# Moving the operands of the small matmuls by 64 bytes in SBUF

## The reference

```
x = x + hgrn2(rmsnorm(x))            # gated linear recurrence, 16 heads of 128, blocks by levels
k, v, F = shared_kv(x)               # keys, values, cumulative forget gates
x = x + fox(rmsnorm(x), k, v, F)     # softmax(q k^T / sqrt(128) + F[t] - F[s], causal) v
h = rmsnorm(x)
x = x + (sigmoid(gr) * rg_lru(conv(h W)) + sigmoid(ga) * dsa_attention(...)) @ w_o
x = x + peer(rmsnorm(x))             # 8 heads, 16 of 128*128 experts each, u[e].x -> gelu -> v[e]
out = rmsnorm(x)
```

## Time and profile before

| | us |
|---|---|
| median of 3 runs | 3218.08 (3217.72 to 3223.16) |
| the profiled execution | 3218.28 |
| its span, first to last instruction | 3216.3 |
| PE busy in the span | 3187.9 (99%), 25285 matmuls |
| DVE busy | 2365.6 (74%) |
| ACT busy | 1686.9 (52%) |
| mean granted TensorE clock | 0.997 |

### The profile page before, as it was taken

One profiled execution on the slowest core, in us unless ns is written; L12 is line 12 of the kernel. 1 busy time (PEld: TensorE's weight loads), 2 busy tenths in 40 slices (PEclk: granted clock), 3 DMA queues, 4 the chain that ended last, 5 costly groups with the idle time before them and its releaser, 6 DMA issues.

```text
span 3216.3 us, 63027 instructions
## 1 busy us (share of the span) xinstructions
PE 3187.9 (99%) x25285; PEld 3028.9 (94%) x25285; DVE 2365.6 (74%) x3779; ACT 1686.9 (52%) x2284; POOL 33.4 (1%) x46
## 2 busy tenths in 40 slices
PE   8999999999999999999999999999999999999998
PEld 8999999999999999999999999998899889987887
DVE  8767667656566776566669998975699558999865
ACT  5444455767775656555544444444444444444444
POOL 4000000000000000000000000000000000000000
PEclk9999999999999999999999999999999999999999
DMA  5444445444445544545454555555555555555554
GB/s 185 159 155 161 152 158 196 158 157 167 161 168 184 190 171 160 189 161 189 169 186 171 185 190 183 181 192 191 190 184 183 195 190 186 181 180 182 183 209 157
DMA packets 99095, 569.94 MB, mean 177 GB/s; under 512 B 9456, under 2 KB 30320, under 8 KB 31600
## 3 DMA queue, kind: packets, MB, share of 16 engines
q1 hardware_dynamic: 98784, 567.06, 49.9%
q10 hardware_dynamic: 144, 0.52, 0.0%
HBM read 565.45 MB, written 2.10 MB: 176 GB/s over the span
## 4 chain that ended last, share of the span: by engine, by line
PE 89%; DVE 7%; DVEq 1%; ACT 1%; issue 1%; DMA 1%; ACTq 0%; POOL 0%; POOLq 0%; SPq 0%
PE bank L583 20%; PE bank L584 20%; PE bank L585 20%; PE bank L1105 7%; PE bank L1107 7%; PE bank L1106 7%; DVE wl L1668 3%; PE bank L1029 1%; PE bank L737 1%; PE bank L940 0%; PE bank L815 0%; PE bank L814 0%; ACT wh L1162 0%; PE bank L686 0%; DMA raw<-w_out_b 0%
## 5 line engine op out<-in xcount | busy, mean ns | idle before, releaser
L584 PE MATMUL bank<-hl,wh 128*128 128x256 f32 x5616 | 1556.9, 277 | 0.0
L583 PE MATMUL bank<-hh,wh 128*128 128x256 f32 x5488 | 1540.5, 281 | 2.8 <-DVE wl L1668 1.7
L585 PE MATMUL bank<-hh,wl 128*128 128x256 f32 x5488 | 1519.7, 277 | 0.0
L1668 DVE TENSOR_TENSOR wl<-raw,wh 128x1024 fp32r<-128x1024 f32 x1052 | 1259.5, 1227 | 327.5 <-ACT wh L1162 319.9
L1162 ACT ACTIVATE wh<-raw 128x1024 fp32r<-128x1024 f32 x1052 | 1051.7, 1050 | 269.9 <-DMA raw<-w_in_a 124.2
L584 PEld LDWEIGHTS bank<-hl,wh 128*128 128x128 f32 x5616 | 1058.0, 188 | 1.9 <-issue 1.7
L583 PEld LDWEIGHTS bank<-hh,wh 128*128 128x128 f32 x5488 | 1034.9, 189 | 7.4 <-issue 2.5
L585 PEld LDWEIGHTS bank<-hh,wl 128*128 128x128 f32 x5488 | 1031.0, 188 | 0.0
L1105 PE MATMUL bank<-wh,ah 128*128 128x512 f32 x1008 | 395.8, 393 | 0.0
L1107 PE MATMUL bank<-wl,ah 128*128 128x512 f32 x1008 | 392.7, 390 | 0.0
L1106 PE MATMUL bank<-wh,al 128*128 128x512 f32 x1008 | 392.3, 389 | 0.0
(11 more groups left out here) (417 smaller groups left out, 3181.8 us busy)
## 6 DMA issues: line engine op xcount, KB each, us to landing
raw<-peer_u SPq DMA_DIRECT2D x128, 1024.0 KB, 4.9
raw<-peer_v SPq DMA_DIRECT2D x128, 1024.0 KB, 4.9
raw<-w_in_c SPq DMA_DIRECT2D x64, 1024.0 KB, 4.9
raw<-w_in_a SPq DMA_DIRECT2D x63, 1024.0 KB, 4.9
raw<-w_kv SPq DMA_DIRECT2D x32, 1024.0 KB, 4.9
raw<-w_in_b SPq DMA_DIRECT2D x32, 1024.0 KB, 4.9
raw<-w_out_a SPq DMA_DIRECT2D x16, 1024.0 KB, 4.9
raw<-w_out_b SPq DMA_DIRECT2D x16, 1024.0 KB, 5.0
```

The source lines that it names most:

```text
L583: eng.matmul(out, h_[:, k, :], high[:, k, :], start=(k == 0), stop=False)
L584: eng.matmul(out, h_[:, k, :], low[:, k, :], start=False, stop=False)
L585: last = eng.matmul(out, low_rows(c, k), high[:, k, :], start=False, stop=(k == KC - 1))
L1668: eng.tensor_tensor(low_half_out(c, half), raw_half(c, half), high_half(c, half).bitcast(F32), ALU.subtract).then_inc(lo_ready, 1)
```

## The change

No instruction is added, taken away or put elsewhere in the order; only the places of tiles in SBUF change. Six pads of 64 bytes stand ahead of groups of tiles (levels' keys; their totals; stage A's values; F's queries and probabilities; F's values; C's probabilities, queries and gate weights), four more ahead of qi, qp, gates_b and iota_h, and two older pads are made shorter by as much, so that ul_c and uh_q stay where they were modulo 128. fqry, prob_f and probT_f move next to qT_f; qT_c, wa and wx move behind probT_c.

```
@@
+        sb_in(m, "KL_offset", [P, 16])
         KL = [sb_in(m, f"KL{n}", [P, W2]) for n in range(LEVELS + 1)]
+        sb_in(m, "TL_offset", [P, 16])
         TL = [sb_in(m, f"TL{n}", [P, W2 >> n]) for n in range(LEVELS)]
@@
+        sb_in(m, "v_a_offset", [P, 16])
         v_a = sb_in(m, "v_a", [P, NT, G])
@@
-        fqry = sb_in(m, "fqry", [P, T])
         fkey = sb_in(m, "fkey", [P, T])
@@
         kT_f = sb_in(m, "kT_f", [P, 2, T])
+        sb_in(m, "held_f_offset", [P, 16])
         qT_f = sb_in(m, "qT_f", [P, 2, T])
+        fqry = sb_in(m, "fqry", [P, T])
+        prob_f = sb_in(m, "prob_f", [P, 2, SC])
+        probT_f = sb_in(m, "probT_f", [P, 2, SC])
+        sb_in(m, "v_f_offset", [P, 16])
         v_f = sb_in(m, "v_f", [P, NT, G])
@@
-        prob_f = sb_in(m, "prob_f", [P, 2, SC])
-        probT_f = sb_in(m, "probT_f", [P, 2, SC])
@@
-        wa = sb_in(m, "wa", [P, 2, P])
-        wx = sb_in(m, "wx", [P, 2, P])
@@
+        sb_in(x, "qi_offset", [P, 16])
         qi = sb_in(x, "qi", [P, 2, W2])
@@
-        sb_in(x, "ul_c_offset", [P, 40])
+        sb_in(x, "ul_c_offset", [P, 24])
@@
-        qT_c = sb_in(m, "qT_c", [P, 2, T])
         kT_c = sb_in(m, "kT_c", [P, 2, T])
@@
         prob_c = sb_in(m, "prob_c", [P, 2, SC])
+        sb_in(m, "held_c_offset", [P, 16])
         probT_c = sb_in(m, "probT_c", [P, 2, SC])
+        qT_c = sb_in(m, "qT_c", [P, 2, T])
+        wa = sb_in(m, "wa", [P, 2, P])
+        wx = sb_in(m, "wx", [P, 2, P])
@@
+        sb_in(r, "qp_offset", [P, 16])
         qp = sb_in(r, "qp", [P, 2, 2, T])
@@
-        sb_in(x, "uh_q_offset", [P, 32])
+        sb_in(x, "uh_q_offset", [P, 16])
@@
+        sb_in(m, "gates_b_offset", [P, 16])
         gates_b = [sb_in(m, f"gates_b{n}", [P, TG, 2, BJ], F16) for n in range(2)]
+        sb_in(m, "iota_h_offset", [P, 16])
         iota_h = sb_in(m, "iota_h", [P, P], F16)
```

## The result

| | before | after |
|---|---|---|
| median us | 3218.97 (3217.72 to 3223.16, 6 runs) | 3236.03 (3234.43 to 3238.0, 6 runs) |
| profiled execution, its span | 3218.28, 3216.3 | 3238.0, 3236.0 |

The ratio is 1.0051, 95% interval 1.0038 to 1.0064: the change makes the kernel 0.5% slower, 17 us. The forecast was 3207.5, faster, with a range from 3204 to 3229.

What follows compares the result with a forecast made beforehand. PE, busy for 99% of the span, was taken to bound the kernel through its rate from start to start. 2.6 + 8.0 = 10.6 us off 3218.08 gave 3207.5, range 3204 to 3229.

Steps and rivals of the forecast that it cites:

- (f): ah and al move by 128 bytes, sum_h, osq_a and uh_a by other amounts; effect on matmul rate taken as 0.
- (a): Small fp32 matmuls, 864 of them: 3 ns less each once their operands lie apart modulo 128; 2.6 us off.
- (b): Stretches behind c_values: probT_c going from 64 to 0 brings 1776 matmuls to the fast rate; 8.0 us off.
- nine places: Places in a loop, nine or so, from which the rule on tile places was drawn; held as likely, no more.
- (c): Behind f_values: probT_f goes from 0 to 64, wh's place; bounds -0.4 to +1.5 us, taken as 0.
- (d): Behind a_values and L972: only stationary v_a or qT_c moves; taken as 0, if slow 3.0 or 3.5 us on.
- (e): At spread: gates_b goes from 0 to 64, the place of wh and ah; taken as 0 for what follows.
- the rival given for "slower": gates_b on wh's and ah's place makes spread leave the slow rate behind; 3228 to 3235, 18% chance.
- the last sentence: If the slow rate is entered by timing, any stretch may change, even behind untouched tiles; no size given.

## Why the prediction was wrong

*(f), ah and al.* This step failed, and with it the sign: the term was put at 0. It took the equal rate of V (both tiles on one place) and of the other products (64 bytes between) as proof that distance does not matter to fp32r matmuls, and "their distance changes all the time" as the reason, which no row showed (and V's moving tile has four times the columns of a load, not two). Both were at their own best place, and the two best places are different. The rows held no third distance for either shape. It also counted places modulo 128, the grid that the change keeps, where the rate repeats after 256 bytes. Measured: +5.6 ns for each matmul of V0, V1 and V3 and +3.9 in V2, +15.9 us, in place of 0. Why the distance sets the rate, no run shows.

*(a), the small fp32 matmuls.* The bound of 0 was the truth: 112.5 ns and loads of 192 ns at 64 bytes as at 0; other distances were not tried. The forecast had 2.6 us. (Its count of 864 leaves out the 192 matmuls of L741, without a reason given.)

*(b), behind c_values.* That the slow rate is a state, that a place decides whether it is entered here, and that it is worth 8.0 us, held (a place alone brought 7.5 us with 0 of 37 slow). The rule was wrong: it looked at the last moving tile and the next load, and the stationary v_c is what counts. The change moved probT_c and left v_c at 64, and got -0.7 in place of -8.0, which alone takes 7.3 us off the forecast's gain of 10.6. The prediction called its nine places "not nine independent trials"; it drew a rule from two of them all the same, though c_values and uv could both have told of another tile.

*(c), behind f_values.* Its upper bound came, +1.0 against the 1.5 given. Before, f_values hands on what it finds: in the kernel before and nine others with F's old places, as many units were slow behind it as behind the transposes ahead of it (2 to 5 of 7). With F's new places it is 7 of 7 in both kernels that have them, against 2 of 7 ahead.

*(d) and (e)* held in rate: no unit behind a_values, L972 or `spread` turned slow with the change. `spread` was the rival given for "slower", with 3228 to 3235, and the time is near to that by another way: its condition, gates_b on the place of wh modulo 128, was met, and 0 of 96 units were slow. Modulo 256 gates_b lies 128 bytes from wh, as v_c does from wh where it leaves the slow rate; gates_b on wh's very place was not tried.

*U0* was foreseen only in the last sentence, that a slow rate may be entered by timing. No operand of U0 moved against another. Over all profiles with hh and hl in their old places, 0, 1, 3, 7 or 24 of its 29 units were slow, and 24 also where just v_c and probT_c had moved (192). The traces narrow it down. U0 ends in one run of 1056 matmuls, in which PE waits three times for weights that DVE has still to split (wl), and its next start comes 0.2 to 1.3 us after the last one. In 14 profiles, 42 such waits, the rate turned slow at 7 of them and fast again at 3, and nowhere between. The last of the three waits, first in the kernel before and then with v_c moved alone:

```profile
1913.98 0.28 PE L585 MATMUL bank<-hh,wl 128*128 128x256 f32 x1
1915.31 0.36 PE L583 MATMUL bank<-hh,wh 128*128 128x256 f32 x1 [1.05 <-DVE wl L1668]
...
1916.77 0.28 PE L583 MATMUL bank<-hh,wh 128*128 128x256 f32 x1
...
1920.51 0.28 PE L583 MATMUL bank<-hh,wh 128*128 128x256 f32 x1
...
1905.64 0.28 PE L586 MATMUL bank<-hh,wl 128*128 128x256 f32 x1
1906.97 0.36 PE L584 MATMUL bank<-hh,wh 128*128 128x256 f32 x1 [1.05 <-DVE wl L1669]
...
1908.10 0.28 PE L584 MATMUL bank<-hh,wh 128*128 128x256 f32 x1
...
1911.99 0.28 PE L584 MATMUL bank<-hh,wh 128*128 128x256 f32 x1
```

Both came to the wait at the fast rate, and the wait is the same. Behind it 33 matmuls take 3.74 us in the first, 113.3 ns each, and 3.89 us in the second, 117.9. In the profiles of the changed kernel and of v_c and probT_c at 192 the run was slow from its first matmul and PE never waited in it: 124.5 us, where the kernel before takes 122.3 with its waits. So a slow U0 costs less than its rate, since the waits go. What starts the slow rate behind the transposes, and which way a wait turns it, stays open. It adds to the differences between single runs of like kernels, as do OF's 13 units and the clock in the first turn of A.

The Trainium skill ("SBUF — State Buffer", SBUF: two separate sides) says that PE never waits on anyone there. No run here tests whether another engine's access slows PE. But the places of PE's own two operands change its rate by 2.5% in V and by 5 to 6% in the others. The Trainium skill ("TensorE: Matmul & The Clock Gate", Part 2, Step-by-step) gives the weight load a read port of its own, which takes nothing from the running matmul. By that the places could not matter; here they do, and the measurement decides.

## What to carry to other kernels

Where matmuls follow each other without a wait, write down the place of the stationary and of the moving tile modulo 256 bytes for the groups with the most matmuls, and move nothing ahead of them without putting those back: here 128 bytes in front of one pair of tiles cost more than all the rest could bring. Measure the best distance for each shape by itself. And where one matmul has two rates from start to start in one trace at one clock, look at what stands ahead of the slow stretch: a 64-column matmul or another place of the small operand there may be worth more than the small matmuls are. Test such steps together as well as alone: here two that each gave 0.3% gave 0.1% together.

## What the runs showed of the hardware

The distance modulo 256 bytes, stationary tile's place less the moving one's, sets the rate of back-to-back fp32r matmuls: 512 columns, 226.7 ns at 0 and 231.5 to 233.0 at 64, 128 and 192; 256 columns, 113.3 at 64, some 119 to 120 at 0 and 128, with 192 not measured.

256-column matmuls at their best distance have two rates, 113.3 and 117.8 ns. In OC they kept the slow one for 768 matmuls, in the changed kernel's U0 for 1056. Inside U0's long run the rate changed at waits of PE alone (10 of 42). A pace ends the slow one mostly, not always: behind uv it stayed in 8 of 8 turns, and OF was slow behind its pace in 3 of 16 profiles.

Which one starts behind `c_values` depends on the place of the stationary v_c modulo 256, with wh at 192: slow at 64 and fast at 128, for probT_c at 64 and at 128; with both at 192 it was slow in the first of eight turns alone.
